# The opening by feature chunk: shift and scale weights in eight pieces, four projection blocks accumulated chunk by chunk

## The reference, cut to what matters

```
mod = silu(c) @ w_mod[0] + b_mod[0]        # 9 x 1024 numbers, the same for c_ctx
m[0], m[1] = shift, scale                  # the first 2048 columns of w_mod[0]
u = rms(h, norm_w) * (1 + m[1]) + m[0]     # per feature, latent and context apart
g, up = split(u @ w_gu)                    # 1024 -> 2 x 2816
h = h + 0.5 * m[2] * ((silu(g) * up) @ w_down)
```

## Time and profile before

| | us |
|---|---|
| median of 3 runs | 1755.82 |
| the profiled execution, its own time | 1756.91 |
| its span, first to last instruction | 1755.1 |
| TensorE busy | 1687.6 (96%) |
| VectorE busy | 1082.3 (62%) |
| ScalarE busy | 613.9 (35%) |

### The profile page before, as it was taken

One profiled execution on the slowest core, in us unless ns is written; L12 is line 12 of the kernel. 1 busy time (PEld: TensorE's weight loads), 2 busy tenths in 40 slices (PEclk: granted clock), 3 DMA queues, 4 the chain that ended last, 5 costly groups with the idle time before them and its releaser, 6 DMA issues.

```text
span 1755.1 us, 24815 instructions
## 1 busy us (share of the span) xinstructions
PE 1687.6 (96%) x8955; PEld 1405.1 (80%) x8955; DVE 1082.3 (62%) x1642; ACT 613.9 (35%) x909; POOL 79.3 (5%) x144
## 2 busy tenths in 40 slices
PE   3999999999998999999999999999999999899999
PEld 1888888887785778888888878888888788589999
DVE  2877777436558667777753277777423376665554
ACT  3422222124525543222222252222222363554443
POOL 0000000000001000000000000000000000000000
PEclk9999999999999999999999999999999999999999
DMA  9466555422221025655552226665323324045554
GB/s 369 135 190 192 183 189 180 144 96 68 89 96 48 25 72 180 188 186 183 188 168 96 97 97 191 183 187 183 107 96 96 96 87 138 17 144 180 183 185 149
DMA packets 69719, 249.23 MB, mean 142 GB/s; under 512 B 7424, under 2 KB 8448, under 8 KB 69504
## 3 DMA queue, kind: packets, MB, share of 16 engines
q1 hardware_dynamic: 51200, 180.83, 32.2%
q0 software_dynamic: 18432, 67.12, 12.0%
HBM read 246.87 MB, written 1.05 MB: 141 GB/s over the span
## 4 chain that ended last, share of the span: by engine, by line
PE 90%; DVE 6%; ACT 2%; SPq 1%; issue 1%; DMA 1%; DVEq 0%; ACTq 0%
PE ps L1007 29%; PE ps L1008 28%; PE ps L1009 28%; PE ps L1058 1%; DVE shared_b L720 1%; PE ps L1192 1%; DMA raw<-wstream 1%; DVE wlo L609 1%; DVE nmax L905 1%; PE ps L1219 1%; DVE xl L706 1%; SPq L280 1%; ACT prob L511 1%; PE ps L1144 0%; ACT whi L349 0%
## 5 line engine op out<-in xcount | busy, mean ns | idle before, releaser
L609 DVE TENSOR_TENSOR wlo<-raw,whi 128x1024 fp32r<-128x1024 f32 x320 | 392.0, 1225 | 585.3 <-ACT whi L349 583.4
L1007 PE MATMUL ps<-xh,whi 128*128 128x512 f32 (+1 forms) x1880 | 682.4, 363 | 23.4 <-DVE xl L706 18.3
L349 ACT ACTIVATE whi<-raw 128x1024 fp32r<-128x1024 f32 x320 | 339.6, 1061 | 1022.8 <-PE ps L1009 1006.2
L1008 PE MATMUL ps<-xl,whi 128*128 128x512 f32 (+1 forms) x1880 | 665.3, 354 | 0.0
L1009 PE MATMUL ps<-xh,wlo 128*128 128x512 f32 (+1 forms) x1880 | 664.4, 353 | 0.0
L1007 PEld LDWEIGHTS ps<-xh,whi 128*128 128x128 f32 x1880 | 359.5, 191 | 87.6 <-issue 31.0
L1008 PEld LDWEIGHTS ps<-xl,whi 128*128 128x128 f32 x1880 | 361.0, 192 | 48.8 <-issue 3.8
L1009 PEld LDWEIGHTS ps<-xh,wlo 128*128 128x128 f32 x1880 | 360.6, 192 | 47.6
L634 DVE SCALAR_TENSOR_TENSOR shared_a<-wm,cs,shared_a 128x512 f32<-128x512 f32 x448 | 307.6, 748 | 0.0
L1007 PE MATMUL ps<-ah,whi 128*128 128x512 f32 (+1 forms) x704 | 255.9, 364 | 0.0
L1008 PE MATMUL ps<-al,whi 128*128 128x512 f32 (+1 forms) x704 | 255.4, 363 | 0.0
(11 more groups left out here) (109 smaller groups left out, 818.2 us busy)
## 6 DMA issues: line engine op xcount, KB each, us to landing
raw<-wstream SPq DMA_DIRECT2D x320, 512.0 KB, 3.5
wm<-wmod POOLq DMA_DIRECT2D x128, 512.0 KB, 3.7
wm<-wmod SPq DMA_DIRECT2D x3, 2048.0 KB, 20.8
h<-x_t SPq DMA_DIRECT2D x1, 2048.0 KB, 11.7
wm<-wmod SPq DMA_DIRECT2D x2, 1024.0 KB, 20.5
K<-cols SPq DMA_DIRECT2D x1, 1195.0 KB, 14.4
out_t<-h SPq DMA_DIRECT2D x8, 128.0 KB, 2.5
K<-cols SPq DMA_DIRECT2D x1, 268.5 KB, 2.9
```

Source lines behind the costliest of these rows:

```text
L349: act.activation(whi[:, n % SPL, :, :].rearrange("p a b -> p (a b)"), raw[:, s, :], ACT.Copy)\
L609: dve.tensor_tensor(wlo[:, n % SPL, :, :].rearrange("p a b -> p (a b)"), raw[:, n % RAW, :], whi[:, n % SPL, :, :].rearrange("p a b -> p ( ...
L1007: pe.matmul(out_ap, hi_w, hi_x, start=start, stop=False)
L1008: pe.matmul(out_ap, hi_w, lo_x, start=False, stop=False)
```

## The change

The weights of shift and scale come as `wfirst`: eight pieces of 1 MB, piece d holding what makes the 128 shift and 128 scale numbers of feature chunk d. SP issues piece 0 first, blocks 0 and 1, piece 1, blocks 2 and 3, pieces 2 to 7, and then the late constants. GpSimd's two early pieces wait for piece 6. For each chunk TensorE makes rows (`opening_rows`, 16 products), ScalarE copies them, TensorE turns them (`opening_sums`), VectorE and ScalarE make this chunk of the normalized input for both streams, and TensorE adds this chunk's part to all four of blocks 0 to 3, in banks 0 to 3 (`opening_blocks`). Five blocks are split ahead, blocks 2 to 4 into places of their own (`ohi`, `olo`). The diff, cut to its core:

```diff
+AHEAD = 5
-                  ("eps", 1), ("sel", 8), ("ones", P),
+                  ("eps", 1), ("sel", 4), ("ones", P),
...
+        def early(n, i):
+            return isinstance(i, int) and i == 0 and n < AHEAD
+
+        def high(n, i=0):
+            return ohi[:, n - SPL, :, :] if n >= SPL and early(n, i) else whi[:, n % SPL, :, :]
...
         def xstep(m, d, s):
-            return XT[m] + DC * s + d + 1
+            return 2 * d + s + 1 if m == 0 else XT[m] + DC * s + d + 1
...
@@ SP
+            first(0)
             for n in range(RAW):
                 sp.dma_start(raw[:, n, :], wstream[n]).then_inc(raw_in[n], 16)
                 if n == 1:
-                    sp.dma_start(K[:, EARLY:NCOL], cols[:, EARLY:NCOL]).then_inc(cols2_in, 16)
+                    first(1)
+            for d in range(2, DC):
+                first(d)
+            sp.dma_start(K[:, EARLY:NCOL], cols[:, EARLY:NCOL]).then_inc(cols2_in, 16)
@@ GpSimd
+            pool.wait_ge(wf_in[DC - 2], 16)
@@ ScalarE
+            def rows_copy(d):
+                act.wait_ge(rows_done, d + 1)
+                if d >= 1:
+                    act.wait_ge(cols_sum, d)
+                act.activation(mrows[:, :], ps[:, 6, 0:P], ACT.Copy).then_inc(rows_out, 1)
+
+            def chunk_start(d):
+                for s in range(2):
+                    g = xstep(0, d, s)
+                    act.wait_ge(xt_done, g)
+                    act.activation(xh[:, d, s * S:(s + 1) * S], xt[:, (g - 1) % 4, :], ACT.Identity,
+                                   bias=modc[:, 0, d, s:s + 1]).then_inc(xh_done, 1)
...
+            rows_copy(0)
             split(0)
             split(1)
-            norm(0)
+            norm_root(0)
+            split(2)
+            rows_copy(1)
+            chunk_start(0)
+            split(3)
+            for d in range(1, DC):
+                if d + 1 < DC:
+                    rows_copy(d + 1)
+                chunk_start(d)
+                if d == 3:
+                    split(4)
@@ VectorE
             split(0)
-            dve.wait_ge(rows_done, 1)
-            dve.tensor_copy(wm0_rows[:, :], ps[:, 5, :]).then_inc(rows_out, 1)
+            chunk_columns(0)
             split(1)
-            dve.wait_ge(mod_sum, START_UNITS)
...
-            norm(0)
+            chunk_x(0)
+            split(2)
+            chunk_low(0)
+            split(3)
+            for d in range(1, DC):
+                chunk_columns(d)
+                chunk_x(d)
+                chunk_low(d)
+                if d == 3:
+                    split(4)
@@ TensorE
+            def opening_rows(d):
+                pe.wait_ge(wf_in[d], 16)
+                if d >= 1:
+                    pe.wait_ge(rows_out, d)
+                for k in range(DC // 2):
+                    for q in range(4):
+                        c = 4 * (q % 2) + k
+                        ins = pe.matmul(ps[32 * q:32 * q + 2, 6, 0:P], cs[:, 2 * c:2 * c + 2], wf[:, d, c, q // 2, :],
+                                        start=k == 0, stop=k == DC // 2 - 1)
                 ins.then_inc(rows_done, 1)
+
+            def opening_sums(d):
+                pe.wait_ge(rows_out, d + 1)
+                ins = pe.matmul(ps[:, 7, 4 * d:4 * d + 4], mrows[:, :], col("sel", 0, 4), start=True, stop=True)
...
+            def opening_blocks(d, blocks):
+                pe.wait_ge(xl_done, xstep(0, d, 1))
+                for n in blocks:
+                    if d == 0:
+                        pe.wait_ge(lo_done, n + 1)
+                    ins = three(ps[:, n, :], high(n)[:, d, :], lowp(n)[:, d, :], xh[:, d, :], xl[:, d, :],
+                                d == 0, d == DC - 1)
+                    if d == DC - 1:
+                        ins.then_inc(block_done, 1)
...
+            opening_rows(0)
+            opening_sums(0)
             norm_stat(0)
-            mod_start()
+            for d in range(DC):
+                if d + 1 < DC:
+                    opening_rows(d + 1)
+                opening_blocks(d, (0, 1))
+                if d + 1 < DC:
+                    opening_sums(d + 1)
+                opening_blocks(d, (2, 3))
```

More of the change, by code:

```diff
@@ L173, in program @@
         cols2_in = sem("cols2_in")
-        wm0_in = [sem(f"wm0_in{p}") for p in range(PAIRS + 1)]
+        wf_in = [sem(f"wf_in{d}") for d in range(DC)]
         rows_zero = sem("rows_zero")
@@ L273, in _, with first @@
             sp.dma_start(h[:, :, :], x_t.rearrange("(c p) t -> p c t", p=P)).then_inc(x_in, 16)
[L274 to L281, removed]
+            def first(d):
+                sp.dma_start(wf[:, d, :, :, :].rearrange("p k a n -> p (k a n)"), wfirst[d]).then_inc(wf_in[d], 16)
+            first(0)
             for n in range(RAW):
@@ L345, in split @@
                 act.wait_ge(raw_in[s], i * (16 * k) + 16 * (n // RAW + 1))
-                if n >= SPL:
+                if n == AHEAD and isinstance(i, int):
+                    act.wait_ge(block_done, AHEAD % SPL + 1)
+                elif not early(n, i):
                     act.wait_ge(block_done, i * (4 * k) + (n - SPL + 1))
-                act.activation(whi[:, n % SPL, :, :].rearrange("p a b -> p (a b)"), raw[:, s, :], ACT.Copy)\
+                act.activation(high(n, i).rearrange("p a b -> p (a b)"), raw[:, s, :], ACT.Copy)\
                     .then_inc(hi_done, 1)
             def split_next(n, i=0, k=0):
-                if n + SPL < NB:
+                if n + SPL < NB and not early(n + SPL, i):
                     split(n + SPL, i, k)
@@ L439, in norm @@
                     act.activation(rstd[:, a], lnv[:, a], ACT.Exp, scale=-0.5).then_inc(rstd_done, 1)
+            def norm(m):
+                norm_root(m)
                 l, st = divmod(m, 3)
@@ L608, in split @@
                 dve.wait_ge(hi_done, i * (4 * k) + (n + 1))
-                dve.tensor_tensor(wlo[:, n % SPL, :, :].rearrange("p a b -> p (a b)"), raw[:, n % RAW, :],
-                                  whi[:, n % SPL, :, :].rearrange("p a b -> p (a b)").bitcast(F32), ALU.subtract)\
+                dve.tensor_tensor(lowp(n, i).rearrange("p a b -> p (a b)"), raw[:, n % RAW, :],
+                                  high(n, i).rearrange("p a b -> p (a b)").bitcast(F32), ALU.subtract)\
                     .then_inc(lo_done, 1)
             def split_next(n, i=0, k=0):
-                if n + SPL < NB:
+                if n + SPL < NB and not early(n + SPL, i):
                     split(n + SPL, i, k)
@@ new lines, in chunk_x @@
+            def chunk_x(d):
+                for s in range(2):
+                    g = xstep(0, d, s)
+                    if d == 0:
+                        dve.wait_ge(rstd_done, s + 1)
+                    if g > 4:
+                        dve.wait_ge(xl_done, g - 4)
+                    dve.scalar_tensor_tensor(xt[:, (g - 1) % 4, :], h[:, d, s * S:(s + 1) * S],
+                                             acol[:, 0, d, s:s + 1], rstd[:, s * S:(s + 1) * S],
+                                             ALU.mult, ALU.mult).then_inc(xt_done, 1)
@@ L984, in _, with chunk_low @@
+            def chunk_low(d):
+                for s in range(2):
+                    g = xstep(0, d, s)
+                    dve.wait_ge(xh_done, g)
+                    dve.scalar_tensor_tensor(xl[:, d, s * S:(s + 1) * S], xt[:, (g - 1) % 4, :],
+                                             modc[:, 0, d, s:s + 1], xh[:, d, s * S:(s + 1) * S].bitcast(F32),
+                                             ALU.add, ALU.subtract).then_inc(xl_done, 1)
             split(0)
-            dve.wait_ge(rows_done, 1)
@@ L1019, in column_block @@
                         pe.wait_ge(*ready[c])
-                    ins = three(ps[:, bank, a:w], whi[:, n % SPL, c, :], wlo[:, n % SPL, c, :],
+                    ins = three(ps[:, bank, a:w], high(n)[:, c, :], lowp(n)[:, c, :],
                                 xh[:, c, a:w], xl[:, c, a:w], c == 0, c == DC - 1)
@@ L1084, in ffn @@
                 F0 = FC * f
-                first_blocks(m, n0)
-                for i in range(GU // 4):
+                if m:
+                    first_blocks(m, n0)
+                for i in range(0 if m else 1, GU // 4):
                     for e in range(2 if i == 0 else 0, 4):
@@ L1352 @@
         "pick": np.repeat((np.arange(64) == 31)[None], P, 0),
-        "sel": np.stack([np.arange(P) == 32 * u + v for u in range(4) for v in range(2)], 1),
+        "sel": np.stack([(np.arange(P) % 32 == v) & (np.arange(P) // 64 == a) for a in range(2) for v in range(2)], 1),
         "cos": np.tile(cos, (2, 1)),
```

65 lines of the change are left out of this document (34 added, 31 removed).

## The result

The changed kernel takes 1765.59 us (median of 4 runs, 1763.72 to 1766.97), the kernel before 1755.82 (1755.58 to 1755.9) on the same chip: ratio 1.0056, 95% interval 1.0041 to 1.0071. It is slower by 9.8 us; the forecast was 1766.7, 10.9 slower. The profiled execution took 1766.97, with a span of 1765.2 (before 1756.91 and 1755.1). TensorE is busy 1692.1 us, 4.5 more.

What follows compares the result with a forecast made beforehand. It took TensorE, nearly idle until 42.39 us, to bound the kernel: a 15.3 us earlier start is given back by chunks taking 46.5 instead of 25.5 and a 5.2 backlog, so 1766.7 us as a median, range 1755 to 1780.

Steps and rivals of the forecast that it cites:

- Start of chunk 0: Opening: first projection product at 27.1 us instead of 42.39, 15.3 earlier, from transfer arrivals and the queues of ScalarE and VectorE.
- A chunk: Opening, each chunk: 6.1 us, from rows 1.1, added wait 1.85, block products 2.72, sums 0.26, switches 0.2.
- rival C: Opening rows: cost goes by pass, 3.6 us a chunk, 17.5 more in all, so 1784 us; chance 0.06.
- Switch of form: TensorE, between narrow and wide products: about 0.1 us each way, 0.2 a chunk.
- The clock: TensorE in the chunks: chunk 0 at half clock, 5.9 us; full clock in later chunks despite 1.85 of idle each.
- rival B: Chunks 1 to 7: the 1.85 us idles make the clock fall, 1775 to 1779 us, all six 1791; chance 0.14.
- Rival D: Opening: added wait and backlog both absent, rows hidden, chunks take 3.0 us each, mark before 60, 1747 us; chance 0.03.
- Rival A: Chunks 1 to 6: ScalarE's copy and high parts hide, saving 1.85 us each, 1755.6 us; chance 0.16.
- `hidden(0)` waits for ScalarE's table load: VectorE in the loop's first pass: waiting for table load and silu makes block 4 start 1.4 us late.
- The other two terms: Block 5: VectorE's late work delays TensorE by 1.8 us at the split and 2.0 at the modulation sums.
- the backlog: VectorE's first modulation pass, no longer done beside blocks 2 and 3, delays TensorE by 5.2 us together, bounds 3 and 7.
- the forecast mark: Block 4's start, late by the whole backlog: 78.8 us against 67.85, 10.9 slower.

Runs made afterwards that it cites:

- e1: Changed kernel with ScalarE making a chunk's two high parts before the copy of the next chunk's rows: 1756.53 us, ratio 0.9999 to the kernel before.
- e7: Changed kernel with e1's order, blocks 2 and 3 split before the root, 8 fillers, modulation half pieces done ahead, GpSimd's pieces after piece 3: 1753.23 us.
- e9: e7 with GpSimd's pieces issued after block 3's transfer and the modulation half pieces behind chunks 2, 4, 5, 6 and 7: 1754.38 us.
- e4: Kernel before, with only GpSimd's two early pieces held back until the last but one shift and scale piece is in: 1753.44 us, ratio 0.9985.
- e6: Changed kernel with each chunk's row products made twice, 32 instead of 16, same result: 1767.47 us, ratio 1.0068 to the kernel before.
- e11: Changed kernel with 24 filler products ahead of the first rows and 8 behind them: 1762.95 us, ratio 1.0042 to the kernel before.
- e12: e9 with block 4 split behind chunk 6 instead of chunk 3, and half pieces behind chunks 2, 3, 4, 5 and 7: 1747.23 us.
- e2: Changed kernel with VectorE doing the loop's first three modulation pieces early, behind the low parts of chunks 2, 4 and 5: 1762.32 us.
- e5: Changed kernel with GpSimd's two early pieces issued at the start, their added wait left out: 1768.56 us, ratio 1.0071 to the kernel before.

## Why the prediction was right

- **Start of chunk 0**: forecast 27.1, measured 26.76. `h` at 10.5 and 10.27, piece 0 at 13.1 and 12.87, the statistic's end at 22.0 and 21.9. The drain rate read from the earlier trace rows held.
- **A chunk**: 6.1 forecast, 5.96 measured (chunks 1 to 6 start at 35.04, 41.01, ... 64.83). The rows are 1.05 (1.1), the wait 1.71 (1.85), the copy 0.28 (0.26). Taking `mod_sums` as the nearest row was right: rival C's 3.6 and the Trainium skill's 81 ns for a load and product pair (TensorE: Matmul & The Clock Gate, Back-to-back issue gap) are not what these column groups show, 1.05/32 = 0.033 us each; the measurement decides.
- **Switch of form**: from the start of the last product, 37.92, to the rows, 38.24, is 0.32, 0.09 over the pitch of 0.23; the product behind the rows has 0.34 to the next, 0.11 over. So 0.2 a chunk as forecast, though the 0.11 is not shown to be the switch: the first product behind a wait has it too where no narrow products came before (79.80, and 80.13 for the next). That a change of tiling mode drains the engine (the Trainium skill, TensorEngine Tiling (Array Packing), Key Properties) agrees with a gap being there, but the 0.16 that a full drain would cost by the forecast's estimate was not seen.
- **The clock**: chunk 0 at half, 5.5 us (5.9 forecast), then full through six idles of 1.71; rival B did not come.
- **Rival D**'s 1747 does not follow from its own terms: eight chunks of 3.0 from 27.1 end at 51.1, which would be 1739. Nothing hung on it; its chance was 0.03 and the time came out slower.
- **Rival A** was decided by ScalarE's order, as forecast: with the copy behind the high parts (e1) the time is 1756.5, where A put it at 1755.6.
- **What failed in size** is "`hidden(0)` waits for ScalarE's table load": the 1.4 ahead of block 4. The load ran at 68.59, before block 1 was done, and block 4 began only 0.2 late. The other two terms measured 1.84 (1.8) and 1.59 (2.0). By the starts the backlog is 0.2 ahead of block 4 and 3.9 from there to the sums, 4.1 where 5.2 stood (a wait delays the next start by up to 0.16 more than its idle, by which a product's record outlasts its pitch): 1.1 of the 2.6 between the forecast mark, +10.9, and the measured +8.3. The other 1.5 are the start (0.3), chunk 0 (0.4) and six chunks 0.14 shorter each.
- The median came within 1.1 us of the forecast partly by luck: the mark was 2.6 us better than forecast, and 1.8 us of scatter behind it hid that in the profiled execution.

## What to carry to other kernels

When stages are cut finer so that an engine can start earlier, list each in-order engine's queue at the new seams: here a copy of 0.28 us ahead of two ready instructions cost near 10 us, and one exchange in that queue gave it back. An earlier start is also spent by covers that go with it: VectorE's side work, the clock across a longer idle, a transfer that long chunks had hidden; remove one wait, profile, and look for the next before adding gains up (e7 and e9 each missed by one such wait). A line of a large change can be a gain by itself (e4), so try the parts alone. And a start read from one trace can differ by 2 us with the same code, so set a small gain by several runs.

## What the runs showed of the hardware

The statistic's last four records take 3.41 us at 18.52 in the changed kernel, though the window 17 to 19 shows PEclk 1.00; in e6 and e11, where TensorE had more to do ahead of them, they take 1.88 under the same 1.00. So in the changed kernel most of them ran at half clock (1.2 GHz), 0.85 us each, and the PEclk of a window that lies before the first change in a trace is not to be relied on here. Idle and clock went together only roughly: six idles of 1.71 kept full clock in the changed kernel, as the one of the earlier trace rows did; one of 1.77 in e12, with TensorE busier before it, was followed by products at half pitch (0.43), and after the 2.96 of e6 (the windows 24 to 26 and 26 to 28 have PEclk 0.98 and 0.50) the first six products were at full clock and the next at half. A longer idle did the same in e2 (3.84, then three products at full clock) and e5 (3.83, then four), while the changed kernel and e1 were at half from the first product behind 3.84 and 3.72. So with the same code the fall comes at different places from one execution to the next. I did not settle what decides between them.

GpSimd's pieces of 0.5 MB take 3.7 us from issue to landing as a median, but in e7, beside SyncE's full queue, VectorE got the first one only at 34.73, 9 us after its issue at 25.6.
